# Lo parts of weights on GpSimd around the norms, four weight items in idle buffers, hi by hi first

## The reference

```python
z = h @ w_in[i]                      # 1024 x 6656: q k v, RNN input, gelu gate, two merge gates
attn = local_attention(rope(q), rope(k), v, sink)        # 8 heads, 2 kv heads, window 128
rnn = (rg_lru(conv(xr), forward) + rg_lru(conv(xr), backward)) * gelu(yr)
merged = sigmoid(ga) * (attn @ w_proj_attn[i]) + sigmoid(gr) * (rnn @ w_proj_rnn[i])
h = layer_norm(DN_ALPHA * h + merged @ w_out[i])
ffn = (gelu(centred_conv(gate)) * val) @ w_down[i]       # gate, val = split(h @ w_up[i]), 3072 wide
ple = sigmoid(h @ w_ple_gate[i]) * (p[i] @ w_ple[i])
h = layer_norm(DN_ALPHA * h + ffn + ple)
```

## Time and profile before

| | us |
|---|---|
| median of 3 runs | 991.38 |
| lowest, highest | 990.43, 995.22 |
| profiled execution | 990.55 |
| its span | 988.4 |
| PE busy in it | 946.8 (96%) |
| DVE busy | 696.6 (70%) |
| ACT busy | 549.9 (56%) |
| POOL busy | 1.4 (0%) |
| mean granted clock of PE | 0.994 of full speed |

### The profile page before, as it was taken

The page is one execution under the profiler, slowest core; times in us unless marked ns, Lnnn a source line. Parts: engine busy times, 40 slices in busy tenths (PEclk is TensorE's granted clock), DMA queues, the critical chain, the costliest instruction groups (busy, mean ns, idle before and its releaser), DMA issues.

```text
span 988.4 us, 13958 instructions
## 1 busy us (share of the span) xinstructions
PE 946.8 (96%) x5824; PEld 845.4 (86%) x5824; DVE 696.6 (70%) x878; ACT 549.9 (56%) x676; POOL 1.4 (0%) x9
## 2 busy tenths in 40 slices
PE   4999999999899999999989999999998999999995
PEld 3998889888689999999769888898886999999984
DVE  6878986777766556556777889877676665556548
ACT  3589988633355444445246999984335444444440
POOL 0000000000000000000000000000000000000000
PEclk9999999999999999999989999999999999999998
DMA  9465436384455555555725455445634756555541
GB/s 312 129 206 165 164 110 210 128 288 159 137 184 189 195 177 185 194 188 181 241 65 191 162 182 166 145 159 201 227 125 154 230 171 200 184 187 184 184 170 42
DMA packets 117757, 174.70 MB, mean 177 GB/s; under 512 B 3904, under 2 KB 78400, under 8 KB 117056
## 3 DMA queue, kind: packets, MB, share of 16 engines
q1 hardware_dynamic: 117408, 173.27, 52.8%
q10 hardware_dynamic: 288, 0.56, 0.1%
HBM read 172.76 MB, written 1.05 MB: 176 GB/s over the span
## 4 chain that ended last, share of the span: by engine, by line
PE 79%; DVE 13%; ACT 5%; issue 2%; DMA 1%; SPq 0%; DVEq 0%; ACTq 0%
PE ring L467 21%; PE ring L468 21%; PE ring L469 21%; DVE sb_w_lo L1033 4%; PE misc L467 4%; PE misc L468 4%; PE misc L469 4%; ACT sb_w_hi L750 2%; PE misc L601 2%; DVE sb_h L1083 1%; PE misc L659 1%; DVE sb_h L1080 1%; PE misc L639 1%; DVE sb_tmp L1204 1%; DVE sb_st L1054 1%
## 5 line engine op out<-in xcount | busy, mean ns | idle before, releaser
L1033 DVE TENSOR_TENSOR sb_w_lo<-sb_raw,sb_w_hi 128x2048 fp32r<-128x2048 f32 (+1 forms) x168 | 363.1, 2162 | 153.5 <-ACT sb_w_hi L750 150.1
L750 ACT CAST sb_w_hi<-sb_raw 128x2048 fp32r<-128x2048 f32 (+1 forms) x168 | 302.4, 1802 | 134.0 <-PE ring L469 72.7
L467 PE MATMUL ring<-sb_x_hi,sb_w_hi 128*128 128x256 f32 x1024 | 291.2, 284 | 3.3 <-DVE sb_w_lo L1033 3.3
L469 PE MATMUL ring<-sb_x_hi,sb_w_lo 128*128 128x256 f32 x1024 | 289.8, 283 | 0.0
L468 PE MATMUL ring<-sb_x_lo,sb_w_hi 128*128 128x256 f32 x1024 | 289.8, 283 | 0.0
L467 PEld LDWEIGHTS ring<-sb_x_hi,sb_w_hi 128*128 128x128 f32 x1024 | 196.5, 192 | 5.1 <-DVE sb_w_lo L1033 4.2
L468 PEld LDWEIGHTS ring<-sb_x_lo,sb_w_hi 128*128 128x128 f32 x1024 | 196.5, 192 | 0.9 <-issue 0.5
L469 PEld LDWEIGHTS ring<-sb_x_hi,sb_w_lo 128*128 128x128 f32 x1024 | 196.5, 192 | 0.0
L467 PE MATMUL ring<-sb_w_hi,sb_x_hi 128*128 128x512 f32 x352 | 142.1, 404 | 7.3 <-DVE sb_w_lo L1033 5.4
L468 PE MATMUL ring<-sb_w_lo,sb_x_hi 128*128 128x512 f32 x352 | 139.2, 395 | 0.0
L469 PE MATMUL ring<-sb_w_hi,sb_x_lo 128*128 128x512 f32 x352 | 138.9, 395 | 0.0
(11 more groups left out here) (132 smaller groups left out, 1148.0 us busy)
## 6 DMA issues: line engine op xcount, KB each, us to landing
sb_raw<-in_w_up_dram SPq DMA_DIRECT2D x48, 1024.0 KB, 5.2
sb_raw<-in_w_in_dram SPq DMA_DIRECT2D x44, 1024.0 KB, 5.2
sb_raw<-in_w_down_dram SPq DMA_DIRECT2D x24, 1024.0 KB, 4.9
sb_raw<-in_w_proj_attn_dram SPq DMA_DIRECT2D x8, 1024.0 KB, 5.1
sb_raw<-in_w_proj_rnn_dram SPq DMA_DIRECT2D x8, 1024.0 KB, 5.1
sb_raw<-in_w_out_dram SPq DMA_DIRECT2D x8, 1024.0 KB, 5.0
sb_raw<-in_w_ple_gate_dram SPq DMA_DIRECT2D x8, 1024.0 KB, 5.1
sb_lnp<-in_ln_dram SPq DMA_DIRECT2D x5, 1024.0 KB, 7.3
```

The lines of the kernel that those rows point to most:

```text
L467: nc.tensor.matmul(dst, lhs[0], rhs[0], start=first, stop=False)
L469: return nc.tensor.matmul(dst, lhs[1], rhs[0], start=False, stop=last)
L750: nc.scalar.copy(w_hi[:, W_OF[n], 0:size], raw[:, slot, 0:size]).then_inc(s_hi_part, 1)
L1033: nc.vector.tensor_tensor(w_lo[:, W_OF[n], 0:size], raw[:, RAW_OF[n], 0:size], hi, ALU.subtract).then_inc(s_split, 1)
```

## The change

The lo part of ten items of each layer is made by POOL: q0 (both items), wo1 (both), ple (both), pg0 (both), g0,0 and d5,1. It counts them on a semaphore of its own, and whoever waits for such an item (PE, and SP before it loads over its raw slot) waits on that one. DVE skips them. Four items leave the slots of `w_hi` and `w_lo` and have their hi and lo parts elsewhere: wo1,1 and ple,1 in the `a` buffers, ple,0 behind p in the `r` buffers, d5,1 in the `r` buffers; the others share the three slots in turn, so that each has its slot three such items later. In the units q0, wo0 and pg0 a part first runs its four matmuls hi by hi, which wait for the hi parts alone, then the four with the weight's lo, then the four with x's lo. The calls that split are moved accordingly, mostly earlier on ACT. `split_order` is a function for another order of the items. The diff, cut:

```diff
+def split_order(l):
+    order = [item for item in items_of(ORDER)]
+    at = order.index(("pg0", 0))
+    ples = [("ple", 0), ("ple", 1)]
+    order = [item for item in order[:at] if item not in ples] + [ples[0], ("pg0", 0), ("pg0", 1), ples[1]] + \
+            [item for item in order[at:] if item not in ples + [("pg0", 0), ("pg0", 1)]]
+    return [(l, name, part) for name, part in order]
+ITEMS = [item for l in range(DEPTH) for item in split_order(l)]
...
-W_OF = [n % W_SLOTS for n in range(len(ITEMS))]
+HOMES = {("wo1", 1): ("a", "pa1"), ("ple", 0): ("r", "pr1"), ("ple", 1): ("a", "wo1"), (f"d{LAST}", 1): ("r", "ple")}
+W_OF = []
+for _l, _name, _part in ITEMS:
+    W_OF.append(None if (_name, _part) in HOMES else sum(w is not None for w in W_OF) % W_SLOTS)
...
-W_FORMER = users_ahead(W_OF)
+W_FORMER = [ITEM[l, HOMES[name, part][1], 1] if (name, part) in HOMES else former
+            for (l, name, part), former in zip(ITEMS, users_ahead(W_OF))]
...
+def by_pool(l, name, part):
+    return name in ("wo1", "ple", "pg0", "q0") or (name, part) in (("g0", 0), (f"d{LAST}", 1))
...
+        def home(n):
+            l, name, part = ITEMS[n]
+            size = item_size(n)
+            if (name, part) not in HOMES:
+                return w_hi[:, W_OF[n], 0:size], w_lo[:, W_OF[n], 0:size]
+            first = 512 if (name, part) == ("ple", 0) else 0
+            pair = (a_hi, a_lo) if HOMES[name, part][0] == "a" else (r_hi, r_lo)
+            return tuple(flat(buf)[:, first:first + size] for buf in pair)
+        def wait_split(eng, n):
+            eng.wait_ge(s_pool_split if by_pool(*ITEMS[n]) else s_split, SPLIT_COUNT[n])
...
-                    sp.wait_ge(s_split, RAW_FORMER[n] + 1)
+                    wait_split(sp, RAW_FORMER[n])
...
+            for n in range(len(ITEMS)):
+                if by_pool(*ITEMS[n]):
+                    pool.wait_ge(s_hi_part, n + 1)
+                    hi, lo = home(n)
+                    nc.gpsimd.tensor_tensor(lo, raw[:, RAW_OF[n], 0:item_size(n)], hi.bitcast(F32),
+                                            ALU.subtract).then_inc(s_pool_split, 1)
...
+            def token_part_hi_first(l, name, hh, t, count):
...
+                pe.wait_ge(s_hi_part, n + 1)
+                pe.wait_ge(s_x_hi, value("x_hi", l, count))
+                for kk, cols in at:
+                    nc.tensor.matmul(bank, x_hi[:, kk, rows], w[0][:, cols], start=kk == 0, stop=False)
+                wait_split(pe, n)
+                for kk, cols in at:
+                    nc.tensor.matmul(bank, x_hi[:, kk, rows], w[1][:, cols], start=False, stop=False)
+                x_ready(l, count)
+                for kk, cols in at:
+                    last = nc.tensor.matmul(bank, x_lo[:, kk, rows], w[0][:, cols], start=False, stop=kk == KT - 1)
...
                         if parts is not None:
-                            x_ready(l, parts + 2 * t + hh + 1)
-                        last = token_part(l, name, hh, t, left)
+                            last = token_part_hi_first(l, name, hh, t, parts + 2 * t + hh + 1)
...
             def hidden_hi(l, j, hh):
+                if j == 0 and hh == 0:
+                    act.wait_ge(s_products, PRODUCT[l, "ple", (1, TT - 1)])
...
-                split_to(l, "wo1", 1)
+                split_until(l, "pg0", 1)
                 x_parts(l, 8, [(0, 0), (0, 1)], 1.0)
-                split_to(l, "ple", 0)
+                split_until(l, "g0", 0)
                 for t in range(TT):
                     out_of(l, "ple", (0, t), ga[:, t, 0:512], ACT.Copy, 0.5)
-                split_to(l, "pg0", 0)
+                x_parts(l, 10, [(1, 0), (1, 1)], 1.0)
                 pg_out(l, 0, 0)
-                x_parts(l, 10, [(1, 0), (1, 1)], 1.0)
                 for t in range(TT):
                     out_of(l, "ple", (1, t), ga[:, t, 512:1024], ACT.Copy, 0.5)
-                split_to(l, "pg0", 1)
+                split_until(l, "g0", 1)
                 pg_out(l, 0, 1)
...
-                split_to(l, "wo1", 0)
                 out_proj(l, 1, 0)
                 all_emptied(dve, l, [("wo1", 0)])
                 norm_stats(l, 1, 0, 1)
                 norm_rest(l, 1, 0)
-                split_to(l, "wo1", 1)
                 x_parts(l, 8, [(0, 0), (0, 1)], 1.0)
                 out_proj(l, 1, 1)
                 all_emptied(dve, l, [("wo1", 1)])
                 norm_stats(l, 1, 1, 1)
-                split_to(l, "ple", 0)
                 norm_rest(l, 1, 1)
-                split_to(l, "pg0", 0)
                 x_parts(l, 10, [(1, 0), (1, 1)], 1.0)
-                split_to(l, "pg0", 1)
```

More of the change, by code:

```diff
@@ L109, in items_of @@
     return items
-ITEMS = [(l, name, part) for l in range(DEPTH) for name, part in items_of(ORDER)]
+MEETS = [(l, name, part) for l in range(DEPTH) for name, part in items_of(ORDER)]
+def split_order(l):
[6 more added lines that the diff above has]
+ITEMS = [item for l in range(DEPTH) for item in split_order(l)]
 ITEM = {item: n for n, item in enumerate(ITEMS)}
@@ L152 @@
     LOADED.append(_at[RAW_OF[_n]])
+def by_pool(l, name, part):
+    return name in ("wo1", "ple", "pg0", "q0") or (name, part) in (("g0", 0), (f"d{LAST}", 1))
+SPLIT_COUNT = []
+_done = {False: 0, True: 0}
+for _item in ITEMS:
+    _done[by_pool(*_item)] += 1
+    SPLIT_COUNT.append(_done[by_pool(*_item)])
 PRODUCT = {}
@@ L157 @@
 _c = 0
-for _n, (_l, _name, _part) in enumerate(ITEMS):
+for _l, _name, _part in MEETS:
+    _n = ITEM[_l, _name, _part]
     _kind = kind_of(_n)
@@ L192 @@
 _open = {}
-for _n, (_l, _name, _part) in enumerate(ITEMS):
-    _kind = kind_of(_n)
+for _n, (_l, _name, _part) in enumerate(MEETS):
+    _kind = UNITS[_name][0]
     if _kind == "down":
@@ L473, in weights @@
                 n = ITEM[l, name, part]
-                pe.wait_ge(s_split, n + 1)
-                return W_OF[n]
+                wait_split(pe, n)
+                return home(n)
             def token_part(l, name, hh, t, left):
-                slot = weights(l, name, hh)
+                w = weights(l, name, hh)
                 if hh == 0:
@@ L485, in token_part @@
                     last = three(bank_of(l, name, t), [x[:, kk, t * P:(t + 1) * P] for x in left],
-                                 [w_hi[:, slot, cols], w_lo[:, slot, cols]], kk == 0, kk == KT - 1)
+                                 [part[:, cols] for part in w], kk == 0, kk == KT - 1)
+                return last
+            def token_part_hi_first(l, name, hh, t, count):
+                n = ITEM[l, name, hh]
+                w = home(n)
+                bank = bank_of(l, name, t)
+                if hh == 0:
+                    pe.wait_ge(s_emptied[RING[l, name, t][0]], free(l, name, t))
+                at = [(4 * hh + k, slice(512 * k, 512 * k + 512)) for k in range(4)]
+                rows = slice(t * P, (t + 1) * P)
+                pe.wait_ge(s_hi_part, n + 1)
+                pe.wait_ge(s_x_hi, value("x_hi", l, count))
+                for kk, cols in at:
+                    nc.tensor.matmul(bank, x_hi[:, kk, rows], w[0][:, cols], start=kk == 0, stop=False)
+                wait_split(pe, n)
+                for kk, cols in at:
[3 more added lines that the diff above has]
+                    last = nc.tensor.matmul(bank, x_lo[:, kk, rows], w[0][:, cols], start=False, stop=kk == KT - 1)
                 return last
@@ L503, in feature_half @@
                         last = three(bank_of(l, name, hh)[:, SEQ * j:SEQ * (j + 1)],
-                                     [w_hi[:, slot, cols], w_lo[:, slot, cols]],
+                                     [part[:, cols] for part in w],
                                      [x_hi[:, k, :], x_lo[:, k, :]], k == 0, k == KT - 1)
@@ L542, in gates_block @@
                             last = three(bank_of(*key)[:, SEQ * d:SEQ * (d + 1)],
-                                         [w_hi[:, slot, at:at + P], w_lo[:, slot, at:at + P]],
+                                         [part[:, at:at + P] for part in w],
                                          [r_hi[:, 2 * b + k, :], r_lo[:, 2 * b + k, :]], k == 0, k == 1)
@@ L547, in ple_part @@
             def ple_part(l, hh, t):
-                slot = weights(l, "ple", hh)
+                w = weights(l, "ple", hh)
                 key = (l, "ple", (hh, t))
@@ L554, in ple_part @@
                     last = three(bank_of(*key), [r_hi[:, k, t * P:(t + 1) * P], r_lo[:, k, t * P:(t + 1) * P]],
-                                 [w_hi[:, slot, cols], w_lo[:, slot, cols]], k == 0, k == 1)
+                                 [part[:, cols] for part in w], k == 0, k == 1)
                 last.then_inc(s_products, 1)
@@ L748, in split_hi, with split_until, split_to @@
                     act.wait_ge(s_products, AFTER_ITEM[W_FORMER[n]])
-                size = item_size(n)
-                nc.scalar.copy(w_hi[:, W_OF[n], 0:size], raw[:, slot, 0:size]).then_inc(s_hi_part, 1)
```

(29 more changed lines are left out.)

42 lines of the change are left out of this document (19 added, 23 removed).

## The result

The changed kernel is slower: 1000.08 us (median of 6 runs, 999.33 to 1002.33) against 991.55 (990.43 to 995.22, 6 runs), ratio 1.0088, 95% interval [1.0072, 1.0104]. Forecast was 983 with a range of 973 to 998, so the sign was wrong and the time lies outside the range. Of the written cases B came true, the one in which GpSimd and DVE exclude each other.

What follows compares the result with a forecast made beforehand. PE bounds the kernel, busy 946.8 of 988.4 us, with 17.6 us of gaps to be had around the norms. Sharing sum 2 x 1.5 + 5.1 + 0 = 8.1 off gave 983 us, range 973 to 998 (own case 977 to 989).

Steps and rivals of the forecast that it cites:

- the sign: Whole kernel: faster, 983 us against the median of 991.38; chance 0.58 of faster by over 5 us.
- B: Rival: DVE steps with two SBUF inputs don't run while GpSimd reads SBUF; sum +6, 997 us; chance 0.33.
- What the two engines do to each other: DVE's two-SBUF-input norm steps beside GpSimd's lo parts: middle taken, twice their time; first norm wins 1.5 instead of 5.2.
- case C: Rival: no mutual cost between GpSimd and DVE; 2 x 5.2 + 5.1 + 1.9 = 17.4 won, 974 us; chance 0.22.
- case A: Forecast's own case, sharing: DVE's two-input steps take twice their time beside GpSimd; 8.1 won, 983 us; chance 0.37.
- GpSimd's lo at 4.6: A 2048-column lo part on GpSimd takes 4.6 us, so PE never waits for it; bounds 2.29 and 9.3.
- the select that was scaled by sixteen: GpSimd row used for the lo part's time: 0.29 us for 128 columns, sixteen times that 4.6 for 2048.
- the 1.66 before g0: First norm of a layer: PE's wait for g0's lo part goes, as the four homes free a slot earlier.
- q0,1's lo: Start of the kernel: this lo part is ready 2.2 us later on GpSimd; start wins 1.9 without mutual cost.
- Hi by hi first at 0: New matmul order in 24 parts: hides 0.3 to 1 us per tile, adds waits; taken as 0, upper end 2.4.
- nothing stays of the 1.9: Under sharing, both tiles' norms at the start lie beside lo parts, so the 1.9 us gain there vanishes.
- the 1.5 for the clock: Under exclusion, first norm of a layer: PE's 4 us wait brings a slow clock stretch costing 1.5 us.

Runs made afterwards that it cites:

- fill runs: GpSimd writes two fills by zero per subtraction: in the changed kernel 973.01 us; as unneeded work beside norms, all lo parts early on DVE, 977.25 us.
- the subtraction that nobody awaits: Kernel with all lo parts early on DVE, plus six GpSimd subtractions of an idle buffer beside the first norms, results unused: 990.27 us, ratio 0.9992.
- the copy below: Kernel with all lo parts early on DVE, plus unneeded GpSimd copies reading one SBUF tensor beside the first norms: 989.1 us, ratio 0.9981.
- all-on-DVE: Changed kernel with all lo parts back on DVE at their old places; homes, ACT calls and hi by hi first stay: 987.12 us, ratio 0.9955.

## Why the prediction was wrong

**The step that failed** is the choice in "What the two engines do to each other": "No row is nearer to one end, so I take the middle: both go on and a DVE step of this kind takes twice its time meanwhile." Shown in its place: the step, which reads two tensors from SBUF, does not go on until GpSimd's instruction is all but over. Sharing would have shown the tiny step at 0.44; it took 4.09. As a term of the sum, what the two engines do to each other was charged with 9.3 us (17.4 of case C less 8.1 of case A) and came to about 27 (973.01 with fills in GpSimd's place, 1000.08 with subtractions). In the fill runs the same step beside a busy GpSimd took 0.22, so holding, not mere company, is what costs, and the subtraction that nobody awaits brought it back.

The Trainium skill (SBUF — State Buffer, section Who interferes with whom) has this rule, and the forecast quoted it and still gave it 0.33. The trace agrees with it on three counts: steps with two SBUF inputs held until the subtraction is over (4.09, 4.52), steps with one not held (0.69 beside GpSimd and away from it), and GpSimd instructions that only write holding nothing (0.22 and 0.74 beside fills). With one kind of instruction, the copy below, the hold ended before GpSimd's record did. The middle between two ends was a choice without a mechanism behind it; a lock has no middle.

**Terms of the sum, one by one.** GpSimd's lo at 4.6: measured 4.49 to 4.61 where it wasn't itself kept waiting, 2.39 to 2.41 for 1024 columns. The value is right and the way to it partly luck: by a straight line through those two lengths 128 columns would take some 0.5 (an estimate), where the select that was scaled by sixteen took 0.29. PE never waited for wo1 or pg0 and the 1.66 before g0 is gone, both right. At the start PE did wait, 2.07 for q0,1's lo: the sum had it ready 2.2 later than before, it was 5.3 later (24.61 against 19.31), since its hi part came 3.0 later behind the held scale step. Hi by hi first at 0: right. Case C's whole sum, 17.4: 17.5 with fills, whose items are 0.9 shorter. Case A worked again by its own rule gives 257.4 for the first tile's steps (257.7 in the text) and about 269.2 for the second's (268.3): small slips, which don't turn its sign.

**Case B against the trace.** Its times in layer 0's first norm are close. Less the 3.0 us that the start lost, the first tile's step is let go at 255.4 (forecast 255.2), the second's at 269.0 (268.4), and g0 starts at 283.1 (281.3, or 282.8 with the 1.5 for the clock). In all it was too mild: it had 2.8 to 4.3 a layer in the first norms, and 4.6 and 3.7 were measured. It had 1 won at the start, and 3.0 were lost: the scale step of the first tile, held 3.1 (3.88 less 0.75), and the tiny one of the second, held 3.65 (3.87 less 0.22), were seen in case A ("nothing stays of the 1.9") and not carried over to B. Between the layers it had 0 and 2.1 were won, although the engines took turns as B says and the first tile was indeed late: its second half is turned 2.4 us later from g0 than before (505.51 less 286.09, 495.56 less 278.49). The second tile was 0.6 earlier, and the matmuls behind it took 1.5 less, at the upper clock level where before they ran at the lower for a while (granted clock 0.93 over the 24.0 us to q0's end, 0.85 over 22.9 before). The all-on-DVE run wins 1.9 there in another way, with the second tile 2.7 earlier and no better clock (0.85). So the other edits (the order on ACT, the home of d5,1) can win about as much there, hi by hi first alone doesn't (237.70 against 237.48), and the larger part of the changed kernel's 2.1 is the clock's, which B had not put in. Sum by B 6, measured in the profiled executions 999.33 - 990.55 = 8.8.

**What the change is made of**, from the runs: GpSimd's lo parts would bring about 14 us if they held nothing (987.12 to 973.01, with items 0.9 us shorter), and cost 13 as they are (987.12 to 1000.08). The 27 us between are the exclusion with the slower clock that its waits bring, but for what the shorter items win (at the start PE waits 0.8 for such an item with fills and 2.07 with subtractions). In the first norm of layer 0, where the stage is 9.8 longer than with fills, the held time is 3.9 + 0.5 + 4.4 = 8.7; a clock of 0.87 for 26.4 us, 3.4 us lost, is in the same stage against 1.00 with fills. These two overlap with waits that PE had anyway and are not to be added.

**Left open.** How each of the other edits shares in the 4 us of the all-on-DVE kernel wasn't tried one by one, but for hi by hi first (none). Its start is 2.3 us longer than before, against which the rest wins 3.4; with the clock changing level from one kernel to the next there, a microsecond or two of any start is not explained by the edits (32.22, 31.44, 33.61 and 33.52 in kernels that do the same there).

## What to carry to other kernels

Before work is given to GpSimd, list DVE's instructions that have two SBUF inputs in the stretch where it will run, tiny ones on one column too, and charge each path that runs through one of them up to the whole of GpSimd's instruction, 4.6 us here, not a share; a GpSimd instruction that reads SBUF belongs beside DVE steps that read PSUM or one tensor. Try first whether DVE's own idle time takes the work: here that brought 13 us where the offload lost 9. And where a rule says "exclusive" and no row contradicts it, a forecast by the middle of two bounds has no ground.
